# The choice of rows for the second head, placed among the dots of the first head

## What is computed

```python
def peer_ffn(h, w_q, sub_keys, u_tab, v_tab):
    ...
        q = (xb @ w_q).reshape(PEER_BLOCK, PEER_HEADS, 2, PEER_HALF)
        s = jnp.einsum('thpd,pkd->thpk', q, sub_keys).astype(jnp.float32)
        s1, i1 = lax.top_k(s[:, :, 0], PEER_TOPK)
        s2, i2 = lax.top_k(s[:, :, 1], PEER_TOPK)
        ...
        top_s, pos = lax.top_k(cand_s, PEER_TOPK)
        idx = jnp.take_along_axis(cand_i, pos, axis=-1)
        wts = jax.nn.softmax(top_s, axis=-1).astype(xb.dtype)
        act = jax.nn.gelu(jnp.einsum('thkd,td->thk', u_tab[idx], xb)) * wts
        return jnp.einsum('thk,thkd->td', act, v_tab[idx])
```

## Time and profile before

| | |
|---|---|
| time, median of 3 runs | 3756.42 us |
| time of the profiled execution | 3756.87 us |
| its span in the profile | 3755.1 us |
| PE busy | 3277.3 us, 87% |
| DVE busy | 2530.7 us, 67% |
| ACT busy | 1754.4 us, 47% |
| POOL busy | 866.2 us, 23% |
| DMA, mean rate | 310 GB/s |

### The profile page before, as it was taken

How to read it: one execution, slowest core, us unless ns; L and a number is a source line. 1 busy time by engine, 2 the same in 40 slices (tenths; PEclk the granted TensorE clock), 3 DMA queues, 4 the chain that set the end, 5 groups by cost and what they waited for, 6 DMA issues and landing times. The chain is left out here.

```text
span 3755.1 us, 38649 instructions
## 1 busy us (share of the span) xinstructions
PE 3277.3 (87%) x13100; PEld 2066.9 (55%) x13100; DVE 2530.7 (67%) x5118; ACT 1754.4 (47%) x3817; POOL 866.2 (23%) x778
## 2 busy tenths in 40 slices
PE   6878888887898899787778777789999999999998
PEld 3444444432354444356322222289888978988896
DVE  2587778777877787556776676566665657666555
ACT  2344445444654655452444444345454545555453
POOL 0033444444443454300444444200000000000000
PEclk8999999999999999988899999989999999999999
DMA  9979999999999999952999999765654555565453
GB/s 397 367 295 418 418 418 404 418 415 420 411 397 417 420 416 421 412 200 87 404 422 421 421 419 421 330 199 168 186 189 156 185 167 162 167 184 185 158 185 117
DMA packets 280470, 1163.50 MB, mean 310 GB/s; under 512 B 31144, under 2 KB 33704, under 8 KB 175824
## 3 DMA queue, kind: packets, MB, share of 16 engines
q0 software_dynamic: 110592, 805.36, 51.8%
q1 hardware_dynamic: 169296, 355.45, 28.7%
q10 hardware_dynamic: 384, 0.23, 0.0%
HBM read 1159.79 MB, written 1.15 MB: 309 GB/s over the span
## 5 line engine op out<-in xcount | busy, mean ns | idle before, releaser
L84 PE MATMUL psum<-rows,diag 128*128 128x512 f32 x3072 | 1487.9, 621 | 325.5 <-ACT diag L2121 320.3
L2077 DVE CUSTOM_DVE_ANT_0 rows<-rows,h 128x1024 f32<-128x1024 f32 x768 | 938.9, 1224 | 488.1 <-DMA rows<-in_p_uv,place 479.5
L84 PEld LDWEIGHTS psum<-rows,diag 128*128 128x128 f32 x3072 | 560.4, 194 | 1166.7 <-ACT diag L2121 657.5
L1973 POOL DMA_INDIRECT rows<-in_p_uv,place x768 | 862.3, 1123 | 1446.6 <-PE psum L84 1118.6
L3116 DVE TENSOR_TENSOR weights_low<-landing,weights_high 128x1024 fp32r<-128x1024 f32 x400 | 488.3, 1224 | 393.0 <-ACT weights_high L2737 392.2
L2737 ACT CAST weights_high<-landing 128x1024 fp32r<-128x1024 f32 x400 | 417.7, 1047 | 571.6 <-PE psum L84 389.1
L2108 ACT ACTIVATE acted<-dots 128x1 f32<-128x1 f32 x768 | 155.2, 202 | 910.4 <-DVE dots L2077 906.9
L84 PE MATMUL psum<-weights_high,hT_high 128*128 128x512 f32 x832 | 353.2, 424 | 14.3 <-DVE h L692 6.8
L2121 ACT ACTIVATE diag<-ident,weight 128x128 f32<-128x128 f32 x768 | 308.5, 402 | 70.7 <-ACT weight L2114 0.7
L84 PE MATMUL psum<-weights_high,hT_low 128*128 128x512 f32 x832 | 326.2, 392 | 0.0
L84 PE MATMUL psum<-weights_low,hT_high 128*128 128x512 f32 x832 | 326.2, 392 | 0.0
(11 more groups left out here) (438 smaller groups left out, 3968.7 us busy)
## 6 DMA issues: line engine op xcount, KB each, us to landing
landing<-in_w_in SPq DMA_DIRECT2D x192, 512.0 KB, 3.9
landing<-in_w_ff SPq DMA_DIRECT2D x128, 512.0 KB, 4.3
landing<-in_w_mod SPq DMA_DIRECT2D x48, 1024.0 KB, 8.8
landing<-in_a_w_in SPq DMA_DIRECT2D x64, 256.0 KB
landing<-in_w_br SPq DMA_DIRECT2D x32, 512.0 KB, 4.0
rows<-in_p_uv,place POOLq DMA_INDIRECT x768
lat_landing<-in_b_w_in SPq DMA_DIRECT2D x48, 256.0 KB
landing<-in_a_w_out SPq DMA_DIRECT2D x32, 256.0 KB
```

What stands on the lines that cost most here:

```text
L84: return k.nc.tensor.matmul(out, lhsT, rhs, start=first, stop=last)
L1973: k.nc.gpsimd.indirect_dma_start(rows[:, n % ROW_RING, :], None, k.given["p_uv"], bass.IndirectOffsetOnAxis(place[:, g % 4, c:c + 1], 0))\
L2077: V.tensor_tensor_reduce(u, u, token, 1.0, 0.0, ALU.mult, ALU.add, dots[:, g % 4, c:c + 1]).then_inc(dots_done, 1)
```

## The change

The pick of group 1 is taken out from ahead of the loop in both mixtures. In the loop, group 0's steps now carry the picks of groups 1 and 2 one behind the other, four steps to a dot instead of two. `shares` of group 1 moves from behind dot 1 to behind dot 10, and on ACT exp of group 1 moves from ahead of the loop to behind step 8. The wait for the copied scores ahead of the first mixture's loop stays.

```diff
@@ dve_first_picks
         yield 164
 
         dve.wait_ge(copied[1], 4)
-        first_pick(1)
@@ second_mix.vector
         dve.wait_ge(copied[0], 1)
-        for head in range(2):
-            first_pick(head)
+        first_pick(0)
         copy_scores(dve, V.tensor_copy, (2, 4, 6))
@@ experts.vector
         for g in range(G):
-            picking = pick(dve, step, g + 2) if g + 2 < G else iter(())
+            if g == 0:
+                picking = chain(pick(dve, step, 1), pick(dve, step, 2))
+            else:
+                picking = pick(dve, step, g + 2) if g + 2 < G else iter(())
...
                 if n == 0:
                     shares(dve, step, 0)
-                if c == 1 and g + 1 < G:
+                if c == (10 if g == 0 else 1) and g + 1 < G:
                     shares(dve, step, g + 1)
-                next(picking, None)
-                next(picking, None)
+                for _ in range(4 if g == 0 else 2):
+                    next(picking, None)
                 aside(n)
@@ experts.scalar
         asked(act, 0)
-        asked(act, 1)
         for n in range(G * TK):
...
             aside(n)
+            if n == 8:
+                asked(act, 1)
             if c == TK - 1 and g + 2 < G:
                 asked(act, g + 2)
```

More of the change, by code:

```diff
@@ L9 @@
 from collections import namedtuple
+from itertools import chain
 from contextlib import ExitStack, contextmanager
```

## The result

The changed kernel takes 3760.01 us (median of 22 runs, 3756.01 to 3763.88); the kernel before, run beside it, 3755.7 us (22 runs, 3750.69 to 3758.18). The ratio is 1.0014, 95% interval 1.0008 to 1.0020: **slower by some 5 us, between 3 and 7.5** (the medians differ by 4.3), where 2 us faster was forecast. It is inside the range and inside 0.2%, but on the other side. The span of the profiled execution is 3759.5 us.

What follows compares the result with a forecast made beforehand. The prediction took DMA engines with nothing to move as what bounds the mixtures. 3756.9 + 2 (first mixture) - 4 (second) = 3754.9, against the median 3754.4; it said 3754.5 us, range 3748 to 3761.5.

Steps and rivals of the forecast that it cites:

- what bounds the mixtures: Both mixtures: only time in which the DMA engines have nothing to move counts; a row costs 2.49 us.
- The standstill of 8.8 us: First mixture, behind dot 0's first four steps: DVE waits for u until 237.4, 8.8 us.
- pick work of 8.2 us: First mixture, at dot 1: 8.2 us of the second pick still to do, making later dots slip.
- 0.75 us a dot: First mixture, DVE full from 240 to 270: dot j slips by 0.75 x (j - 1) us, 8.2 from dot 12.
- +2 us: First mixture's loss: row 19's bytes come some 2.3 us after the queue empties; +2 us, between 0 and +8.2.
- So at 280.0 it is empty: First mixture: gather 19 goes out at 280.0, when the gather queue has moved 19.0 rows, rows 0 to 18.
- DVE catches up, so it happens once: First mixture, dots 12 to 15: no pick steps there, so DVE recovers and the +2 us loss is not repeated.
- PE's time per row: First mixture: gathers follow their slipped dots as before; 18 moves from 270.06 to 276.8, 19 from 271.77 to 280.0.
- Rival 2: First mixture: DVE's standstill paid in full, 8.2 us, if no gather is outstanding from about dot 2; 3760.6 us, chance 0.13.
- -4 us: Second mixture's gain: earlier dot 0 and gather 8 close the DMA hole behind row 7; -4 us, between 0 and -7.4.
- the edit on ACT: Both mixtures: exp of head 1 behind dot 8, with table loads, priced at nothing; 3 us each without cover.
- rival 4: Second mixture: gathers 2 to 7 issue slower beside copies and a dot; 3768 or 3761 us, chance 0.04.

Runs made afterwards that it cites:

- e2: Changed kernel's edits bound to the first mixture, the second left as in the kernel before: 3759.7 us against 3756.0, ratio 1.0012.
- e5: Kernel before plus one useless DVE statistics instruction behind each of dots 1 to 11 of the first mixture: 3762.0 us against 3756.0, ratio 1.0017.
- e3: Changed kernel, but the first mixture's whole second pick stands directly behind dot 0, in DVE's wait for u: 3754.9 and 3755.1 us, ratios 0.9996 and 0.9998.
- e12: Built from e3: in both mixtures the whole second pick directly behind dot 0, then two steps a dot: 3753.7 us against 3755.3, ratio 0.9997.
- the ballasts: Kernel before plus useless DVE instructions in the first mixture, for 4.4, 8 or 16 us of lag: 3756.3, 3762.0 and 3769.8 us.
- e10: e2 plus two useless products on PE ahead of its wait for row 4 of the first mixture: 3763.9 us against 3755.3, ratio 1.0020.
- e4: Kernel before with only the later exp and shares of head 1, in both mixtures, picks left ahead of the loop: 3755.8 us against 3755.7, ratio 0.9999.
- e6: Kernel before plus one useless DVE instruction behind each of dots 1, 3, 5, 7, 9, 11 of the first mixture: 3756.3 us against 3755.7, ratio 1.0000.

## Why the prediction was wrong

- **Right: what bounds the mixtures.** Time without bytes decides. The edits change the stages by what the DMA's windows lose or win, and a dot that is early in itself buys nothing (e2 against e5).
- **Right: where the loss comes from.** The standstill of 8.8 us was 8.70, and 8.49 in e2; pick work of 8.2 us was to be pushed back, and dot 12 of e2 is 8.7 us late. e3 fills the wait, and the loss is gone. In e2 gather 19 came 62.8 us behind the first, against 280.0 - 217.7 = 62.3 in the prediction. That closeness is partly luck: by the prediction's own 0.75 us a dot, dot 11 slips by 7.5 and gather 19 comes at 279.3, not 280.0.
- **Failed: "+2 us", the reserve of the first mixture.** It measured 5.8 us in e2, 6.8 and 7.1 in the changed kernel. The step that failed is "So at 280.0 it is empty". The 19.0 rows moved by 280 are the kernel before's; taking them over says that gathers 12 to 18, each late by itself, cost nothing, because each still goes out while another is moving. In e2 18.0 rows were moved by 280: dips from 258 to 278 had lost 2.6 us already, and the hole at 280, the only one in the sum, 1.7. e12 shows by itself that a gather just issued does not keep the rate, and the ballasts show that all but 0.6 to 1.6 us of a lag is paid. By the measure of these runs, which the prediction did not have, 8.2 us of lag cost 5.3 to 7.6.
- **A second miss in the same term:** "DVE catches up, so it happens once". DVE does, from 8.7 us at dot 12 to 4.0 at dot 20, but PE is full behind it, and gather 28 is 8.0 us late.
- **A part of the first:** PE's time per row was taken from before. From dot 4 to gather 12, which needs row 4 used, 6.3 us pass in e2 and 4.5 before: 1.8 us that the dots' slip doesn't give. e10, with PE on its upper level there, has 4.5 again.
- **Rival 2 (0.13) was near for two reasons that cancel.** Its 3760.6 fits the 3760.0, and its row, 8.1 of 9 rows moved at 246, was a row to go by. But its condition, no gather outstanding, did not hold, its 8.2 us is over the 5.8 to 7.1 measured, and the gain that it shares, 4, is over the one measured.
- **Mis-sized: "-4 us", the gain of the second mixture.** The hole closed, dot 0 came 8.7 us earlier (7.4 predicted), gather 8 10.6 (over 9). The mean of the five profiles with the changed second mixture against that of the eight with the untouched one is 3.3 us less at gather 28, 2.5 at gather 128 and 2.4 at the last; against the one profile of before the changed kernel has 3.3, 3.0 and 1.9. The hole itself gave 3.8 by the prediction's windows, and the dip at 1806 is no less real for what follows it: 389 GB/s from 1808 to 1810, then 438 and 422. Rounding up to 4 had no row behind it. What takes 0.8 us between gathers 28 and 128 isn't known.
- **Right: the edit on ACT costs nothing that shows** (e4), and gathers beside dots don't starve the DMA (rival 4: the longest is 1.63 us among gathers 1 to 7).
- **Readings that don't come out as written, and change little:** the slices are counted from 0, and slice 25 moves 330 GB/s, not 400. The gathers' 51.8% is a share of the whole span, not of the DMA's own time, of which it is 64%. With 2.7 us a row, rows 0 to 15 are through at 271.8 and not 271.4, so a row is seen 1.7 us behind its bytes, and the 3.6 us would be 4.0.
- **Together:** 6.8 to 7.1 lost, 1.9 to 2.4 won, 4.4 to 5.2 us slower by the stages; the ratio gives 3 to 7.5.

## What to carry to other kernels

Moving work off a critical start into a stream helps only where the stream's engine has no other wait behind it: look at what stands next in that engine's order, and whether the moved work was filling that wait. When a ring feeds a DMA that bounds, count as reserve only transfers whose bytes are ready to move, that is issued at least one issue-to-bytes time ago; a busy share of 1.0 does not tell whether one row is in hand or five. If both are close, put in a ballast instruction of known length: a run or two show how much lag a stage really covers. And a lag is not over when the engine that had it has caught up: look at the engines that wait for it.

## What the runs showed of the hardware that was not expected

From the issue of an indirect gather of 1 MB into an empty queue to its bytes some 2.5 us pass (the kernel before, issue at 1798.59; 82 GB/s from 1800 to 1801, 254 in the next microsecond, 418 from 1802), as long as the row itself takes at 421 GB/s. With only one gather moving and the next just issued the rate is 217 GB/s over two microseconds (e12). Behind 3.28 us of idle time PE, granted 0.50 and then 0.75, made a row's products in 2.8 us instead of 1.98 (e2), inside a window whose mean clock was 0.89. And kernels whose instructions are the same up to a point differed in the clock granted ahead of it: the same 16 products took 5.35 and 5.59 us in e4 and e6, and 3.91 in the kernel before.
